# The opening of a two-layer hybrid diffusion trunk: ScalarE copies the modulation rows and takes the norm's root before it splits the first weights

## The chip, the cores and the metric

The kernel runs on one core of a Trainium2 chip. The metric is the device time of one execution in microseconds (us), the median of three runs. The trace is of one execution. Each engine works through its own instructions in program order, and a semaphore wait holds up everything that stands behind it on that engine. In names of rows, PE is TensorE (PEld its weight loads), ACT is ScalarE, DVE is VectorE, POOL is GpSimd, SP is SyncE, which here only issues DMAs; a trailing q is an engine's DMA queue or sequencer.

## The reference

Two layers (`DEPTH` = 2) over 256 context and 512 latent tokens of width 1024. What matters for this change is how layer 0 begins:

```python
sh1x, sc1x, ... = split_cols(silu(c) @ w_ada[l] + b_ada[l], (D_MODEL,) * 6)   # the same of c_ctx
hx = modulate(rms_norm(x, norm_mix_pre[l]), sh1x, sc1x)     # h * (1 + scale) + shift
hc = modulate(rms_norm(h_ctx, norm_mix_pre[l]), sh1c, sc1c)
y_x, y_c = mixing_layer(hx, hc, w_in[l], ...)               # begins with hx @ w_in, hc @ w_in
```

Everything is float32. Behind it stand the three mixers (gated DeltaNet, latent attention, HGRN2), the output projection and an MLP with squared ReLU.

## The kernel before

Activations lie transposed: 8 blocks (`KB`) of 128 features on the partitions by 768 tokens (`TOK`). `X` (residual) is the stream, `Hm` (modulated) its normalised and then modulated form. A float32 product is made of three products of two parts each: `high` is the value cast to fp32r, `low` the rest, and high·high, low·high and high·low are summed.

The order on each engine is written by hand, engine by engine, and semaphores join them. The opening of layer 0 goes like this.

- **SP** issues the constants, the inputs, eight 1 MB loads of modulation weights (`ada_first`, four groups of two halves), the masks, the first three 1 MB loads of `w_in` into a ring of three slots (`weights`), and a copy of `X` to memory (`x_kept`).
- **TensorE** transposes the inputs. Then, for each of the four groups of modulation weights, it multiplies both halves by silu(c) (`ada_half`, L742) into a bank of PSUM. Once ScalarE has copied such a group out as a row (`ada_rows`, L1314), `ada_columns` (L749) turns the row into columns. Between these it sums the squares of `X` over the 1024 features with a matrix of ones (`sum_squares`, L702): blocks 0 to 3 behind group 0, blocks 4 to 7 behind group 1. Then comes the first projection, `gemm_parts` of "qkv" 0 (L672), which for each block k of features waits for `q_low_ready` k+1, and before all for `proj_low_ready` 1.
- **ScalarE** squares the eight blocks (L1327), loads the table for Ln and Exp (`root_tables`, L1237), makes the high part of the first `w_in` weights (`proj_high_part(0, 0)`, L1260, which waits until they have landed), copies two modulation rows, takes the root of the norm as Ln and Exp (`inverse_roots`, L1247 and L1252), copies the other two rows and modulates the eight blocks (`modulate`, L1296, two instructions a block), for which it waits for `mods_ready`.
- **VectorE** makes the low part of the first weights (`proj_low_part`, L1649), multiplies the eight blocks of `X` by the root (`norm_input`, L1636), adds the bias to the modulation columns and makes the gain (L1705, L1715, which raises `mods_ready`), then makes `q_low` for each block (`q_low_block`, L1654).
- **GpSimd** casts each modulated block to its high part (`q_high`, L563), on which `q_low` of that block waits.

Behind the opening, every load into the ring waits for the projection that used the slot last, every projection for its weights' low part, and the convolutions for the projections.

Of the kernel before, what the change touches and what calls it, by code (L numbers as in the profile page):

```python
# [13 lines left out]
KB = D // 128  # L14
# [18 lines left out]
ADA_FIRST = 4  # L33
# [18 lines left out]
def landed(n):  # L52

    return 16 * sum(DMAS.get(what, 1) for _, what, _ in LOADS[n % NSLOT:n + 1:NSLOT])
# [19 lines left out]
def number(table, layer, what, i=0):  # L74

    return layer * len(table) + table.index((what, i))
# [18 lines left out]
def trunk_program(nc, x, ctx, c, c_ctx, w_ada, b_ada, norm_mix_pre, norm_mix_post, norm_mlp_pre, norm_mlp_post,  # L95
# [6 lines left out]
    with stack:  # L102
# [41 lines left out]
        ident, ones, bd64 = kf[:, 0, :], kf[:, 1, :], kf[:, 2, :]  # L144
# [51 lines left out]
        def square_buffer(what, i, n):  # L196

            if what in ("norm0", "norm3"):
                return Y[:, i, :]
            if what in ("norm1", "norm2"):  # L200
                return blocks((2 if what == "norm1" else 0) + i // 4)[:, i % 4, :]
            if what == "l2":
                return X[:, i % 4, :]
            return R[:, 4 if what == "grms" else 6, TOK * (n % 4):TOK * (n % 4 + 1)]
# [30 lines left out]
        def proj_width(s):  # L235

            return 1024 if PROJ[s][0] in ("ba", "ckv") else 2048

        def proj_high(s):

            if s < 7:
                z = R_r[:, 3, 0:2048] if s % 2 else S_r[:, :, :].rearrange("p a b -> p (a b)")
            elif s < 17:
                z = S_r[:, :, :].rearrange("p a b -> p (a b)") if s % 2 else R_r[:, 7, 0:2048]
            else:
                z = R_r[:, s - 15, 0:2048]
            return z[:, 0:proj_width(s)]
# [83 lines left out]
        def lo_of(l):  # L331

            return 0 if l < DEPTH - 1 else CTX
# [4 lines left out]
        def segments(lo):  # L338

            return ([(0, CTX, 1)] if lo == 0 else []) + [(CTX, TOK, 0)]  # L340
# [113 lines left out]
        ada_first = R[:, 1:7, :].rearrange("p a b -> p (a b)")[:, 0:2 * ADA_FIRST * 2048].rearrange("p (i n) -> p i n", n=2048)  # L454
# [182 lines left out]
        def _(pe):  # L637
# [7 lines left out]
            def free_pair(l, what, i=0):  # L645

                n = number(UNITS, l, what, i)
                if n >= 4:
                    pe.wait_ge(gemm_evac, n - 3)
                return pair(n)  # L650

            def streams(lo):
                return ([(0, CTX)] if lo == 0 else []) + [(CTX, TOK)]
# [39 lines left out]
            def sum_squares(l, what, n0, n, mat, lo=0, part=None):  # L693

                dst = free_pair(l, what, n0)
                first = number(SQUARES, l, what, 0 if n > 1 else n0)
                for k in (range(n) if part is None else part):
                    pe.wait_ge(sq_ready, first + k + 1)
                    block = k
                    sq = square_buffer(what, block if n > 1 else n0, first + k)  # L700
                    for a, b in streams(lo):
                        last = mm(dst[:, CTX + a:CTX + b], mat, sq[:, a:b], start=(k == 0), stop=(k == n - 1))  # L702
                    last.then_inc(sq_used, 1)
# [35 lines left out]
            def ada_half(half, w, bank):  # L739

                for k in range(4):
                    last = mm(ps[32 * k:32 * k + 32, bank, :], cs[:, 4 * half + k, :], w[:, k, :], start=(half == 0), stop=(half == 1))  # L742
                return last

            def ada_columns(g, row, col):

                pe.wait_ge(ada_row, g + 1)
                for j in range(4):
                    last = mm(ps[:, 7, col + 2 * j:col + 2 * j + 2], row[:, 128 * j:128 * j + 128], sel[:, :], start=True, stop=True)  # L749
                last.then_inc(ada_tr, 1)  # L750
# [17 lines left out]
            for l in range(DEPTH):  # L768
                lo = lo_of(l)
                if l == 0:  # L770
                    pe.wait_ge(cs_ready, 1)
                    pe.wait_ge(xT_evac, 2 * NC)
                    pe.wait_ge(sel_ready, 1)
                    for g in range(ADA_FIRST):
                        for half in range(2):
                            pe.wait_ge(ada_in[2 * g + half], 16)
                            last = ada_half(half, ada_first[:, 2 * g + half, :].rearrange("p (k n) -> p k n", n=512), 2 + g)
                        last.then_inc(ada_out, 1)
                        if g < 2:
                            sum_squares(l, "norm0", 0, KB, ones, part=range(4 * g, 4 * g + 4))  # L780
                        else:
                            ada_columns(g - 2, ada_first[:, 2 * g - 3, :], 8 * g - 16)
                    for g in range(ADA_FIRST - 2, ADA_FIRST):
                        ada_columns(g, ada_first[:, 2 * g + 1, :], 8 * g)
                else:
                    sum_squares(l, "norm0", 0, KB, ones)
                for i in range(3):
# [406 lines left out]
        def _(act):  # L1194
# [59 lines left out]
            def proj_high_part(l, s):  # L1254

                n = LOADS.index((l, *PROJ[s]))
                act.wait_ge(w_in_s[n % NSLOT], landed(n))
                if 2 <= s < 7 or 9 <= s < 17:
                    act.wait_ge(*weights_used(LOADS.index((l, *PROJ[s - 2]))))
                af(proj_high(s), ring[:, n % NSLOT, 0:proj_width(s)], ACT.Copy).then_inc(proj_high_ready, 1)  # L1260
# [28 lines left out]
            def modulate(l, w, A, B):  # L1289

                if w == 0:
                    act.wait_ge(mods_ready, l + 1)
                for b in range(KB):
                    act.wait_ge(xn_ready, 8 * (2 * l + w) + b + 1)
                    for a, e, s in segments(0 if w == 0 else lo_of(l)):
                        last = af(Hm[:, b, a:e], Hm[:, b, a:e], ACT.Identity, bias=B[:, b, s:s + 1], scale=A[:, b, s:s + 1])  # L1296
                    last.then_inc(h_ready, 1)
# [14 lines left out]
            def ada_rows(g, row, bank):  # L1312
                act.wait_ge(ada_out, g + 1)
                af(row[:, 0:512], ps[:, bank, :], ACT.Copy).then_inc(ada_row, 1)  # L1314
# [6 lines left out]
            for l in range(DEPTH):  # L1321
# [5 lines left out]
                    af(square_buffer("norm0", b, 0), X[:, b, :], ACT.Square).then_inc(sq_ready, 1)  # L1327
                if l == 0:
                    root_tables()
                    proj_high_part(0, 0)  # L1330
                if l == 0:
                    for g in range(2):
                        ada_rows(g, ada_first[:, 2 * g + 1, :], 2 + g)
                inverse_roots(l, [("norm0", 0, D, KB, 0)])
                if l == 0:
                    for g in range(2, ADA_FIRST):
                        ada_rows(g, ada_first[:, 2 * g + 1, :], 2 + g)
                modulate(l, 0, A1, mods[:, l, 0:8, :])
                if l == 0:
                    proj_high_part(0, 1)  # L1340
# [264 lines left out]
        def _(dve):  # L1605
# [38 lines left out]
            def proj_low_part(l, s):  # L1644

                at = slot(l, *PROJ[s])
                dve.wait_ge(proj_high_ready, len(PROJ) * l + s + 1)
                w = proj_width(s)
                v.tensor_tensor(ring_r[:, at, 0:w], ring[:, at, 0:w], proj_high(s), ALU.subtract).then_inc(proj_low_ready, 1)  # L1649
# [58 lines left out]
            for l in range(DEPTH):  # L1708
                lo = lo_of(l)

                def gain(dst, b0, at, plus_one):

                    g = vecs[:, 2 * l, at:at + 8].unsqueeze(2).to_broadcast([128, 8, 2])
                    m = mods[:, l, b0:b0 + 8, :]
                    return (v.scalar_tensor_tensor(dst[:, :, :], m, 1.0, g, ALU.add, ALU.mult) if plus_one  # L1715
                            else v.tensor_tensor(dst[:, :, :], m, g, ALU.mult))
                if l == 0:
                    proj_low_part(l, 0)
                    norm_input(l, "norm0", 0)
                    dve.wait_ge(ada_tr, ADA_FIRST)  # L1720
                    add_bias(0, 0, 16, ps[:, 7, 0:32])
                    gain(A1, 8, V_MIXPRE, True).then_inc(mods_ready, 1)
                    dve.wait_ge(mask_in, 16)
                    for b in range(KB):
                        q_low_block(l, b)
                    proj_low_part(l, 1)
                else:
                    gain(A1, 8, V_MIXPRE, True).then_inc(mods_ready, 1)
                    proj_low_part(l, 0)
                    proj_low_part(l, 1)  # L1730
                    rs = roots(l, "norm0")
                    for b in range(KB + 2):
                        if b < KB:
                            v.tensor_tensor(Hm[:, b, :], X[:, b, :], rs, ALU.mult).then_inc(xn_ready, 1)
                        if b >= 2:
                            q_low_block(l, b - 2)
# [414 lines left out]
```

## Time and profile before

| | |
|---|---|
| median of three runs | 2569.98 us (2568.72 to 2570.99) |
| the profiled execution, first to last instruction | 2553.6 us |
| median less this span | 16.4 us |
| TensorE busy | 2404.3 us, 94% of the span |
| VectorE, ScalarE, GpSimd busy | 1343.5, 860.0, 235.1 us |
| mean granted TensorE clock | 0.981 of full |
| first matmul of the first projection starts | 56.98 us into the span |

The span runs from the first to the last instruction; the device time has 16.4 us around it. The profiled execution's own time as a run is not listed, so a change is counted against its span, and the 16.4 us are taken to stay. The busy share of an engine is an average over the whole kernel; what the opening costs is read from the order of events in its first 60 us.

### The profile page before, as it was taken

To read this page: it belongs to the slowest core of one execution; us is meant where nothing else is said; L and a number is where in the kernel's file an instruction comes from. 1 tells how busy PE (TensorE), PEld (TensorE's weight loads), DVE (VectorE), ACT (ScalarE), POOL (GpSimd) and SP (SyncE) were. 2 spreads that over 40 slices of the span, in tenths; PEclk is the share of its full clock that TensorE was granted. 3 is DMA by queue.
4 is the path that set the end of the run, shared out by engine and by line. 5 is a ranking of instruction groups with operands and counts; after the bars stand their busy time and mean duration, and the time that the engine had idled before them with its cause. 6 is when DMAs were issued, how large, how long until landed. Compare 5 with 4: busy or idle time off the path is not lost.

```text
span 2553.6 us, 34253 instructions
## 1 busy us (share of the span) xinstructions
PE 2404.3 (94%) x14914; PEld 2024.6 (79%) x14914; DVE 1343.5 (53%) x1824; ACT 860.0 (34%) x1197; POOL 235.1 (9%) x188
## 2 busy tenths in 40 slices
PE   6999999999989899999999799999998898999997
PEld 4889797888857688888888587878887756788885
DVE  3689652158654362334333578955228564634444
ACT  5374323210254432122223537343210264322223
POOL 2034300000030020000000013400000030000000
PEclk8999999999999999999999899999999999999998
DMA  8213401122220111122221221431220022233331
GB/s 296 58 51 101 148 11 57 56 77 84 73 99 18 50 50 60 57 66 67 66 66 64 85 58 51 133 116 34 66 81 28 15 99 67 66 99 99 99 99 50
DMA packets 159260, 192.83 MB, mean 76 GB/s; under 512 B 18134, under 2 KB 129080, under 8 KB 158599
## 3 DMA queue, kind: packets, MB, share of 16 engines
q1 hardware_dynamic: 154864, 183.84, 22.2%
q10 hardware_dynamic: 3543, 6.43, 0.8%
q8 instruction: 118, 1.93, 0.3%
q0 software_dynamic: 704, 0.37, 0.1%
q14 instruction: 31, 0.25, 0.0%
HBM read 182.19 MB, written 8.44 MB: 75 GB/s over the span
## 4 chain that ended last, share of the span: by engine, by line
PE 80%; DVE 11%; ACT 4%; issue 2%; SPq 1%; DMA 1%; POOL 0%; DVEq 0%; ACTq 0%
PE ps L1178 33%; PE ps L672 18%; PE ps L1147 4%; PE ps L702 3%; PE ps L1019 2%; PE ps L872 2%; PE ps L878 2%; PE ps L1096 2%; DVE region L1961 1%; PE ps L986 1%; PE ps L1164 1%; DVE region L1992 1%; PE ps L659 1%; PE ps L1109 1%; DVE residual L1856 1%
## 5 line engine op out<-in xcount | busy, mean ns | idle before, releaser
L1178 PE MATMUL ps<-region_r 128*128 128x512 f32 (+1 forms) x1536 | 376.3, 353 | 0.0
L1178 PEld LDWEIGHTS ps<-region_r 128*128 128x128 f32 x1536 | 270.6, 188 | 40.9
L1178 PE MATMUL ps<-region_r,weights_r 128*128 128x512 f32 (+1 forms) x768 | 229.6, 353 | 0.0
L1178 PE MATMUL ps<-mixed_r,region_r 128*128 128x256 f32 (+1 forms) x720 | 215.2, 353 | 0.0
L1178 PE MATMUL ps<-modulated_r,region_r 128*128 128x256 f32 (+1 forms) x720 | 215.2, 353 | 0.0
L1178 PE MATMUL ps<-mixed_r,weights_r 128*128 128x256 f32 (+1 forms) x720 | 215.2, 353 | 0.0
L1642 DVE TENSOR_TENSOR weights_r<-weights,region_r 128x2048 fp32r<-128x2048 f32 x64 | 146.4, 2288 | 118.4 <-ACT region_r L1274 118.4
L1178 PEld LDWEIGHTS ps<-region_r,weights_r 128*128 128x128 f32 x768 | 144.3, 188 | 20.6
L2097 DVE TENSOR_TENSOR region_r<-region 128x768 fp32r<-128x768 f32 (+1 forms) x64 | 52.8, 825 | 204.7 <-ACT region L1582 204.7
L672 PE MATMUL ps<-residual_r,weights_r 128*128 128x256 f32 (+1 forms) x576 | 160.4, 346 | 0.0
L1582 ACT ACTIVATE region<-ps,cst 128x768 f32<-128x768 f32 (+1 forms) x64 | 51.1, 798 | 320.8 <-PE ps L1178 311.3
L1019 PEld LDWEIGHTS ps<-region 128*128 128x128 f32 x1120 | 128.2, 191 | 30.9 <-DVE region L1961 22.5
L1178 PEld LDWEIGHTS ps<-mixed_r,weights_r 128*128 128x128 f32 x720 | 135.3, 188 | 19.2
L1178 PEld LDWEIGHTS ps<-modulated_r,region_r 128*128 128x128 f32 x720 | 135.3, 188 | 19.2
L1178 PEld LDWEIGHTS ps<-mixed_r,region_r 128*128 128x128 f32 x720 | 135.3, 188 | 19.1
L1019 PE MATMUL ps<-region 128*128 128x128 f32 (+1 forms) x1120 | 132.7, 276 | 15.0 <-DVE region L1961 15.0
L1274 ACT ACTIVATE region_r<-weights 128x2048 fp32r<-128x2048 f32 x64 | 122.1, 1908 | 0.0
L672 PEld LDWEIGHTS ps<-residual_r,weights_r 128*128 128x128 f32 x576 | 108.2, 188 | 14.6 <-issue 0.2
L1649 DVE TENSOR_TENSOR weights_r<-weights,state_r 128x2048 fp32r<-128x2048 f32 x18 | 41.2, 2291 | 137.7 <-ACT state_r L1260 137.7
L1588 ACT ACTIVATE region<-ps 128x768 f32<-128x768 f32 (+1 forms) x48 | 33.9, 706 | 215.7 <-PE ps L1178 215.7
L672 PE MATMUL ps<-region_r,state_r 128*128 128x256 f32 (+1 forms) x360 | 90.3, 355 | 14.9 <-DVE region_r L1654 12.1
L672 PE MATMUL ps<-region_r,weights_r 128*128 128x512 f32 (+1 forms) x384 | 104.3, 347 | 0.0
(347 smaller groups left out, 4820.1 us busy)
## 6 DMA issues: line engine op xcount, KB each, us to landing
weights<-in_w_mlp SPq DMA_DIRECT2D x64, 1024.0 KB, 5.4
weights<-in_w_ada SPq DMA_DIRECT2D x40, 1024.0 KB, 5.2
weights<-in_w_in SPq DMA_DIRECT2D x34, 1024.0 KB, 5.2
region<-in_w_ada SPq DMA_DIRECT2D x8, 1024.0 KB, 17.0
weights<-in_w_out SPq DMA_DIRECT2D x8, 1024.0 KB, 6.8
x_kept<-residual SPq DMA_DIRECT2D x2, 3072.0 KB, 12.6
region<-decays_kept ACTq DMA_DIRECT2D x4, 1536.0 KB, 10.6
residual<-x_kept SPq DMA_DIRECT2D x2, 3072.0 KB, 10.8
```

The lines of the kernel that those rows point to most:

```text
L672: last = mm(dst[:, CTX + a:CTX + b], w[:, k, m], r[k][:, a:b], start=(k == 0 and w is high and r is r_high), stop=(k == KB - 1 and r is r_ ...
L702: last = mm(dst[:, CTX + a:CTX + b], mat, sq[:, a:b], start=(k == 0), stop=(k == n - 1))
L872: last = mm(ps[:, ci, 128 * h:128 * h + 128], NT[:, ci, h, :], inverse_alternate(ci, size, h), start=True, stop=True)
L878: last = mm(ps[:, ci, 128 * h:128 * h + 128], W[ci][:, h, :], TT_alternate(ci, size, h), start=True, stop=True)
L1019: last = mm(ps[:, bank, first:first + 64 * ne].rearrange("p (e n s) -> p e n s", e=ne, n=blocks_of), HK[d][:, h, 128 * ci:128 * ci + 128], ...
L1096: last = mm(dst[:, CTX + s0:CTX + s1], QH[0:96, h, 128 * qt:128 * qt + 128], KH[0:96, h, s0:s1], start=True, stop=True)
L1147: last = mm(dst[:, CTX + a:CTX + b], w[:, k, m], r[:, a:b], start=(k == 0 and part_of == "low"), stop=(k == 5 and w is low))
L1178: last = mm(dst[:, CTX + a:CTX + b], w[:, k, m], r[:, a:b], start=(k == 0 and r is r_low), stop=(k == KB - 1 and w is low))
L1274: af(w_high[j % 2], ring[:, n % NSLOT, :], ACT.Copy).then_inc(w_high_ready, 1)
L1582: copied(l, what, u, af(hid[:, b, lo:], src, ACT.Relu, bias=zero_col))
L1642: v.tensor_tensor(ring_r[:, at, :], ring[:, at, :], w_high[j % 2], ALU.subtract).then_inc(w_low_ready, 1)
L2097: v.tensor_tensor(hid_high[:, b, lo:], z, z, ALU.mult)
```

## The change

Three functions change, all for layer 0 and all in the order of the work alone: no instruction is added or left out.

```diff
# TensorE
                         last.then_inc(ada_out, 1)
-                        if g < 2:
-                            sum_squares(l, "norm0", 0, KB, ones, part=range(4 * g, 4 * g + 4))
+                        if g == 0:
+                            sum_squares(l, "norm0", 0, KB, ones)
                         else:
-                            ada_columns(g - 2, ada_first[:, 2 * g - 3, :], 8 * g - 16)
-                    for g in range(ADA_FIRST - 2, ADA_FIRST):
-                        ada_columns(g, ada_first[:, 2 * g + 1, :], 8 * g)
+                            ada_columns(g - 1, ada_first[:, 2 * g - 1, :], 8 * g - 8)
+                    ada_columns(ADA_FIRST - 1, ada_first[:, 2 * ADA_FIRST - 1, :], 8 * ADA_FIRST - 8)
# ScalarE
                 if l == 0:
                     root_tables()
-                    proj_high_part(0, 0)
-                if l == 0:
-                    for g in range(2):
-                        ada_rows(g, ada_first[:, 2 * g + 1, :], 2 + g)
+                    ada_rows(0, ada_first[:, 1, :], 2)
                 inverse_roots(l, [("norm0", 0, D, KB, 0)])
                 if l == 0:
-                    for g in range(2, ADA_FIRST):
+                    for g in range(1, ADA_FIRST):
                         ada_rows(g, ada_first[:, 2 * g + 1, :], 2 + g)
+                    proj_high_part(0, 0)
                 modulate(l, 0, A1, mods[:, l, 0:8, :])
# VectorE
                 if l == 0:
-                    proj_low_part(l, 0)
                     norm_input(l, "norm0", 0)
                     dve.wait_ge(ada_tr, ADA_FIRST)
                     add_bias(0, 0, 16, ps[:, 7, 0:32])
                     gain(A1, 8, V_MIXPRE, True).then_inc(mods_ready, 1)
+                    proj_low_part(l, 0)
                     dve.wait_ge(mask_in, 16)
```

ScalarE's instructions from the squares to the first modulated block, before (the splitting of the first weights is the row `state_r<-weights`, the modulation rows are `region<-ps 128x512`, Ln and Exp the two rows of 128x768 with `cst`):

```order
L1327 ACTIVATE mixed<-residual 128x768 x8
L1237 ACT_TABLE_LOAD
L1260 ACTIVATE state_r<-weights 128x2048
L1314 ACTIVATE region<-ps 128x512 x2
L1247 ACTIVATE region<-ps,cst 128x768
L1252 ACTIVATE region<-region,cst 128x768
L1314 ACTIVATE region<-ps 128x512 x2
L1296 ACTIVATE modulated<-modulated,modulation,pre_gain 128x256
```

and in the changed kernel, whose line numbers are one to three lower:

```order
L1326 ACTIVATE mixed<-residual 128x768 x8
L1236 ACT_TABLE_LOAD
L1313 ACTIVATE region<-ps 128x512
L1246 ACTIVATE region<-ps,cst 128x768
L1251 ACTIVATE region<-region,cst 128x768
L1313 ACTIVATE region<-ps 128x512 x3
L1259 ACTIVATE state_r<-weights 128x2048
L1295 ACTIVATE modulated<-modulated,modulation,pre_gain 128x256
```

One row copy and Ln and Exp now stand ahead of the weights, as do the other three row copies; the weights stand directly ahead of the modulation.

VectorE's instructions from the end of the constants to `q_low`, before:

```order
L1701 TENSOR_TENSOR lower_bound<-lb_tmp 128x8
L1649 TENSOR_TENSOR weights_r<-weights,state_r 128x2048
L1636 TENSOR_TENSOR modulated<-residual,region 128x768 x8
L1705 TENSOR_TENSOR modulation<-ps,vecs 128x32
L1715 SCALAR_TENSOR_TENSOR pre_gain<-modulation,vecs 128x16
L1654 TENSOR_TENSOR region_r<-modulated,region_r 128x768 x4
```

and now:

```order
L1698 TENSOR_TENSOR lower_bound<-lb_tmp 128x8
L1633 TENSOR_TENSOR modulated<-residual,region 128x768 x8
L1702 TENSOR_TENSOR modulation<-ps,vecs 128x32
L1712 SCALAR_TENSOR_TENSOR pre_gain<-modulation,vecs 128x16
L1646 TENSOR_TENSOR weights_r<-weights,state_r 128x2048
L1651 TENSOR_TENSOR region_r<-modulated,region_r 128x768 x4
```

The low part of the weights (`weights_r<-weights,state_r`) has moved from ahead of the norm to between the gain and the first `q_low`.

TensorE's instructions from the second half of the sum of squares to the first projection (each block has two matmuls of L702, and an instruction in float32 stands once here and in several passes in the trace), before:

```order
L702 MATMUL ps<-mixed,k_f_sb 128x256
L702 MATMUL ps<-mixed,k_f_sb 128x512
L702 MATMUL ps<-mixed,k_f_sb 128x256
L702 MATMUL ps<-mixed,k_f_sb 128x512
L742 MATMUL ps<-region,silu_c 32x512 x8
L749 MATMUL ps<-row_select,region 128x2 x4
L742 MATMUL ps<-region,silu_c 32x512 x8
L749 MATMUL ps<-row_select,region 128x2 x12
L672 MATMUL ps<-region_r,state_r 128x256
```

and now:

```order
L702 MATMUL ps<-mixed,k_f_sb 128x512
L702 MATMUL ps<-mixed,k_f_sb 128x256
L702 MATMUL ps<-mixed,k_f_sb 128x512
L742 MATMUL ps<-region,silu_c 32x512 x8
L749 MATMUL ps<-row_select,region 128x2 x4
L742 MATMUL ps<-region,silu_c 32x512 x8
L749 MATMUL ps<-row_select,region 128x2 x4
L742 MATMUL ps<-region,silu_c 32x512 x8
L749 MATMUL ps<-row_select,region 128x2 x8
L672 MATMUL ps<-region_r,state_r 128x256
```

Group 1 (one `region,silu_c` row) has moved from the middle of the sum to behind it, and each group's columns (`row_select,region`) now follow one group later, not two.

## Rows read from the trace of the kernel before

**Rows 1.** The page, part 4: the whole span's chain that ended last, by engine.
```profile
PE 80%; DVE 11%; ACT 4%; issue 2%; SPq 1%; DMA 1%; POOL 0%; DVEq 0%; ACTq 0%
```

**Rows 2.** ScalarE's timeline: start, length, instruction, [idle before it <- what ended that].
```profile
21.97 5.98 ACT L1327 ACTIVATE mixed<-residual 128x768 f32<-128x768 f32 x8
27.97 1.28 ACT L1237 ACT_TABLE_LOAD   x1
...
49.24 0.60 ACT L1314 ACTIVATE region<-ps 128x512 f32<-128x512 f32 x1 [2.60 <-PE ps L742]
53.58 9.71 ACT L1296 ACTIVATE modulated<-modulated,modulation,pre_gain 128x256 f32<-128x256 f32 x16 [3.74 <-DVE pre_gain L1715]
```

**Rows 3.** The chain that ended last, in order of time: start us, us, what.
```profile
23.45 2.58 SPq L464
...
28.70 12.79 DMA weights<-in_w_in
...
41.51 1.91 ACT state_r L1260
...
44.40 0.80 ACT region L1247
...
45.22 0.95 ACT region L1252
...
46.19 7.04 DVE modulated L1636 x8
...
53.58 1.31 ACT modulated L1296 x2
...
54.94 0.83 POOL region_r L563
...
55.87 0.97 DVE region_r L1654
...
56.98 77.80 PE ps L672 x432
```

**Rows 4.** TensorE's timeline, 20 to 60 us.
```profile
23.89 5.43 PE L702 MATMUL ps<-mixed,k_f_sb 128*128 128x256 f32 x16
...
31.11 5.43 PE L702 MATMUL ps<-mixed,k_f_sb 128*128 128x256 f32 x16
36.46 1.92 PE L742 MATMUL ps<-region,silu_c 128*32 128x512 f32 x16
43.96 1.87 PE L749 MATMUL ps<-row_select,region 128*128 128x2 f32 x8 [5.57 <-ACT region L1314]
45.76 3.40 PE L742 MATMUL ps<-region,silu_c 128*32 128x512 f32 x16
49.09 2.84 PE L749 MATMUL ps<-row_select,region 128*128 128x2 f32 x24
```

**Rows 5.** DMA issues: the last of w_ada, and x_kept: number, KB each, median us from issue to landing.
```profile
region<-in_w_ada SPq DMA_DIRECT2D x1, 1024.0 KB, 14.2
...
x_kept<-residual SPq DMA_DIRECT2D x1, 3072.0 KB, 16.1
```

**Rows 6.** GpSimd's timeline, 53.5 to 58.2 us.
```profile
56.14 1.38 POOL L563 CAST region_r<-modulated 128x768 fp32r<-128x768 f32 x1 [0.37 <-ACT modulated L1296]
...
57.47 0.83 POOL L563 CAST region_r<-modulated 128x768 fp32r<-128x768 f32 x1
```

**Rows 7.** VectorE's timeline, 56.2 to 60 us.
```profile
57.55 1.54 DVE L1654 TENSOR_TENSOR region_r<-modulated,region_r 128x768 fp32r<-128x768 f32 x1 [0.72 <-POOL region_r L563]
```

**Rows 8.** Busy time and granted TensorE clock (PEclk, 1.00 is full) in stretches.
```profile
core 0: us, PE busy (x) PEld busy (x) DVE busy (x) ACT busy (x) POOL busy (x), PEclk, DMA share, GB/s
...
42.00:44.00 2.00, 0.04 (x1) 0.04 (x1) 0.47 (x1) 2.00 (x3) 0.00 (x0) 0.50 1.10 349
52.00:54.00 2.00, 0.00 (x0) 0.00 (x0) 1.50 (x4) 0.42 (x1) 0.00 (x0) 0.55 0.27 115
...
62.00:64.00 2.00, 2.00 (x12) 1.74 (x11) 2.00 (x3) 2.00 (x4) 2.00 (x2) 0.89 0.03 8
```

## The prediction, made before the changed kernel ran

> **What bounds the kernel now.** I read the chain that ended last, first for the whole span and then for the first 60 us. Over the whole span TensorE holds 80% of it [rows 1], and from 56.98 us on it runs through 432 projection matmuls in one piece of 77.80 us [rows 3]. What the opening decides is thus when that piece starts. The chain ahead of it is: the landing of the first `w_in` weights at 28.70 + 12.79 = 41.49; their high part on ScalarE, 1.91; two row copies, Ln and Exp; the norm on VectorE from 46.19, 7.04; the modulation of block 0 from 53.58, 1.31; GpSimd's cast, 0.83; VectorE's `q_low`, 0.97; then TensorE [rows 3].
>
> The engines' timelines show that Ln had no need to wait for that landing. ScalarE ended the squares at 21.97 + 5.98 = 27.95 and the table load at 29.25, then had nothing to do until 41.51 [rows 2, 3]. TensorE ended the sum of squares at 31.11 + 5.43 = 36.54 and group 2 at 38.38, then stood still for 5.57 us until a modulation row had been copied [rows 4]. Ln stood behind the weights in ScalarE's order, and so did the rows that TensorE waited for.
>
> **The change, part by part.** The arithmetic is the same. I follow the new order with the old durations.
>
> *TensorE.* Group 0 ends as before, and the sum starts at 23.89. Its second half takes 36.46 - 31.11 = 5.35 from start to start [rows 4], so both halves take 10.7 and end at 34.6, with the last result out at 34.7. The squares finish at 27.95, ahead of it. Group 1 runs 34.6 to 36.5 (1.9, as group 2 in [rows 4]). The columns of a group are a third of 24 matmuls in 2.84, so 0.95 [rows 4]. Then: columns 0 to 37.4, group 2 to 39.3, columns 1 to 40.2, group 3 to 42.1, columns 2 to 43.1, columns 3 to 44.0. The last half of group 3 was issued at 23.45 and landed 14.2 later [rows 3, 5], at 37.65, so it is there. Each row is copied while TensorE does something else: row 0 at 29.3, row 1 behind Exp at 36.5, row 2 at 39.3, row 3 at 42.2 to 42.8 (0.60 each [rows 2]).
>
> *ScalarE and the norm.* Ln starts at 34.7, where it started at 44.40. From its start to the norm's are 46.19 - 44.40 = 1.79 [rows 3], so the norm runs 36.5 to 43.6. Now it ends 0.4 ahead of the columns, and these become the later of the two. From the norm's end to the modulation were 53.58 - 53.23 = 0.35 [rows 3]; from 44.05 that gives `mods_ready` at about 44.4. But ScalarE has taken the weights at 42.8 (they landed at 41.49), and for 1.9 they hold the modulation behind them: it starts at **44.65**, 8.9 earlier than 53.58. The weights thus cost 0.25 on the path here; they cost 1.9 before.
>
> *VectorE's low part of the weights* was hidden: it ended under Ln and Exp. Now it stands between the gain and `q_low` 0, and starts with the end of the high part, 44.65 to 44.8. Its duration is not in my rows of the chain, so I bound it by them: 2048 columns where a `q_low` of 768 takes 0.97 [rows 3], hence up to 2.6, and 2.3 when 0.1 of each is a fixed cost. It ends at about 47.1. Before, `q_low` 0 came 55.87 - 53.58 = 2.29 behind the modulation's start; 44.65 + 2.29 = 46.9. Without more, it would now start at 47.1, and the gain at TensorE would be 8.9 - 0.15 = about 8.7.
>
> *The two engines that meet there.* GpSimd's cast of block 0 wants to start at 44.65 + 1.36 = 46.0, in the middle of that low part. The trace shows what such a meeting costs. The cast at 56.14 began during `q_low` 0 (55.87 to 56.84) and took 1.38, where one alone takes 0.83; it ended at 57.52, 0.7 behind the end of the VectorE instruction [rows 3, 6]. And `q_low` 1, at 57.55, took 1.54 against 0.97, because the cast at 57.47 (0.83, to 58.30) had come first [rows 6, 7]. So I take it that one stands until the other has ended. Then cast 0 ends at 47.1 + 0.7 = 47.8, cast 1 follows at once (its block is ready at 44.65 + 2.5), and `q_low` 0, which starts at 47.8, takes the 1.54 of `q_low` 1 and ends at 49.3. TensorE started 56.98 - 56.84 = 0.14 behind that: **49.5**, which is 7.5 earlier. The bounds of this term: nothing, with the gain 8.7 to 8.9; and 1.4, the one I take, as both meetings have a row like them. If a cast lost only the 0.55 that the row shows, it would end at 47.4 and the gain would be 7.9.
>
> The Trainium skill, "SBUF — State Buffer", section "Who interferes with whom", says that a VectorE instruction with two inputs in SBUF and a GpSimd instruction that reads SBUF exclude each other, the second to issue standing until the first has ended. By that rule the cast stands behind the whole 2.3 us low part, not only for the 0.55 of the row, and the sum would be 7.5 and not 7.9. The two casts of the row agree with it, but no row here has a cast behind so long an instruction.
>
> *TensorE's clock.* It was full until 52.2, 0.3 us after TensorE's last matmul, then half (mean 0.55 over 52 to 54), and full again from about 62.4 (mean 0.89 over 62 to 64) [rows 8]. So the first projection ran its first 5.5 us at half clock and lost 2.7. In the new order TensorE stands still from 44.0 to 49.5, 5.5 us against 5.05, so I expect the same fall and the same loss; 0 is my value, with a bound of 1 us either way for when the clock comes back. The gaps ahead of it, which had group 3 at 3.40 and not 1.92 [rows 4], close.
>
> *Behind the opening.* The second `q_low` follows 1.5 after the first, and TensorE takes longer than that per block at half clock, so VectorE doesn't hold it. `x_kept` is issued at 38.41 as before and lands 16.1 later [rows 5], at 54.5; VectorE asks for it behind eight `q_low` and one low part, at 49.3 + 7 x 1.5 + 2.3 = 62. Every later load waits for a projection, so it moves with them. I take the whole 7.5 as passed on.
>
> Sum: 2553.6 - 7.5 = 2546.1 for the span; with the same 16.4 around it, 2562.5 against the median of 2569.98, 0.29% less.
>
> **The rivals.**
> 1. *The meeting costs nothing* (cast and low part run side by side): gain 8.7 to 8.9, 2561.2. Against it stand both long rows of [rows 6, 7]. An earlier return of the clock comes to the same side: up to 2.7 more, were it full from the first matmul. Chance of this side: 0.17.
> 2. *The clock falls during the columns.* The one fall that [rows 8] hold came right behind 24 column matmuls of 2 columns each, on a TensorE that was busy all through them. The new order has such matmuls from 36.5 on, a third of the time. If the clock fell at about 41, group 3 would take up to 1.5 more and the two column steps behind it 0.85 each (43.96 to 45.76 for 8 against 0.95 [rows 4]). Columns 3 would end at 47.2, the modulation start at 47.6 with the low part behind it as before: 3.0 given back, gain 4.5, 2565.5. For the forecast speaks that two thirds of that stretch is full-width work, as ahead of 38.38. Chance 0.14.
> 3. *The change doesn't do what it says.* The gain in the opening is made, and a later wait takes it back, so that the time stays at 2570. That needs an event tied to the clock on the wall and not to the projections; I found none but `x_kept`, which has 7 us to spare. Chance 0.05.
> 4. *Slower: the weights' landing.* ScalarE now waits for `w_in` 0 directly ahead of the modulation, and the eight blocks stand behind that wait. Landed at 41.49, it costs nothing before 42.8; from there each us costs one. It decides from 42.8 + 7.5 = 50.3 on, 8.8 later than it landed. With a landing of 52.8 the kernel would take 2572.5 or more, if its earlier form did not share the delay. The transfers ahead of it are the same. Chance 0.04.
>
> **How the numbers follow.** Forecast (gain 6.5 to 8.5): 0.60. Rivals: 0.17, 0.14, 0.05, 0.04. What a measurement of this kernel can tell from no change is about 0.2%, 5.1 us. Faster by more: 0.60 + 0.17 + a little of rival 2 = 0.79. Within: 0.17. Slower: 0.04. The range goes down to 2560.0 (rival 1 with some of the clock) and up to 2566.5 (rival 2 with 1 us of spread between runs, which was 2568.72 to 2570.99).
>
> **What would show it.** Right: the first L672 matmul at 49.5 (49 to 50), the norm from 36.5, the modulation from 44.65, a cast of 1.7 or so that ends 0.7 behind the low part, full clock from 34 to 44, and all later events earlier by one and the same amount. Wrong: a cast 0 of 0.83 (rival 1), a group 3 of over 2.5 us (rival 2), a wait after 60 us that is longer than before (rival 3), or a wait of ScalarE for `w_in` (rival 4).

## The result: faster by more than was forecast, and outside the range

Over 22 runs of each, the changed kernel took 2554.36 us (median; 2543.17 to 2571.28) and the kernel before 2569.35 us (2555.23 to 2585.39). The ratio is 0.9945, 95% interval 0.9925 to 0.9966: 14 us less, where 7.5 were forecast, and below the range's lower end of 2560.0. Counted over all runs of this study (162 of before with a mean of 2566.5, one more of 3488.25 us at a clock of 0.647 left out; 70 of the changed kernel with a mean of 2555.2) it is **11.3 us, with 2.4 either way** (1.96 times the root of the summed squares of the standard errors, 0.7 and 1.0). That interval takes every run as independent. The sets that the runs came in differ by more than this allows (below, "Both kernels again"); counted over the means of the seven sets of before and the five of the changed kernel, it is 11.6 with 3.5 either way.

The opening in the trace of the changed kernel went nearly as predicted. Its page begins and its chain by engine reads:

```profile
span 2547.5 us, 34253 instructions
...
PE 81%; DVE 11%; ACT 3%; issue 2%; DMA 1%; SPq 1%; POOL 0%; DVEq 0%; ACTq 0%
```

The chain that ended last (start us, us, what), beside [rows 3]:

```profile
28.82 13.63 DMA weights<-in_w_in
42.50 1.79 issue
44.30 1.30 ACT modulated L1295 x2
45.60 0.05 issue
45.65 1.76 POOL region_r L563
47.46 0.04 issue
47.50 1.48 DVE region_r L1651
48.98 0.14 issue
49.12 77.04 PE ps L672 x432
```

Ln, Exp and the norm are gone from the chain. The piece of 432 projection matmuls starts at 49.12 and not at 56.98, 7.86 earlier, and takes 77.04 (77.80 in [rows 3]). It is shorter because the clock came back sooner behind its start: it was 0.50 over 48 to 52 us, 0.76 over 52 to 54 and 1.00 over 54 to 56, so that some 3.9 us ran at half clock, where [rows 8] give 5.5 before.

ScalarE's timeline shows what took their place:

```profile
28.57 0.60 ACT L1313 ACTIVATE region<-ps 128x512 f32<-128x512 f32 x1
33.84 0.90 ACT L1246 ACTIVATE region<-ps,cst 128x768 f32<-128x768 f32 x1 [4.67 <-PE ps L702]
...
41.39 0.60 ACT L1313 ACTIVATE region<-ps 128x512 f32<-128x512 f32 x1 [2.24 <-PE ps L742]
42.48 1.91 ACT L1259 ACTIVATE state_r<-weights 128x2048 fp32r<-128x2048 f32 x1 [0.49 <-DMA weights<-in_w_in]
44.30 9.68 ACT L1295 ACTIVATE modulated<-modulated,modulation,pre_gain 128x256 f32<-128x256 f32 x16
```

Ln now waits for the sum of squares, as it should, and the weights still end the chain, since they landed at 42.45 here. The wait is 0.49 us: rival 4's mechanism, in a small form. VectorE's timeline:

```profile
35.81 7.04 DVE L1633 TENSOR_TENSOR modulated<-residual,region 128x768 f32<-128x768 f32 x8 [19.23 <-ACT region L1251]
43.24 0.19 DVE L1702 TENSOR_TENSOR modulation<-ps,vecs 128x32 f32<-128x32 f32 x1 [0.39 <-PE ps L749]
...
44.42 2.29 DVE L1646 TENSOR_TENSOR weights_r<-weights,state_r 128x2048 fp32r<-128x2048 f32 x1 [0.78 <-ACT state_r L1259]
```

and TensorE's, beside [rows 4]:

```profile
23.21 10.59 PE L702 MATMUL ps<-mixed,k_f_sb 128*128 128x256 f32 x32
33.73 1.92 PE L742 MATMUL ps<-region,silu_c 128*32 128x512 f32 x16
35.58 1.05 PE L749 MATMUL ps<-row_select,region 128*128 128x2 f32 x8
...
39.40 1.92 PE L742 MATMUL ps<-region,silu_c 128*32 128x512 f32 x16
41.26 1.95 PE L749 MATMUL ps<-row_select,region 128*128 128x2 f32 x16
```

Group 3 takes 1.92 (3.40 in [rows 4]). The clock over 34 to 44 us was 1.00 (the columns are those of [rows 8]):

```profile
34.00:44.00 10.00, 9.20 (x80) 4.89 (x72) 7.41 (x10) 4.98 (x6) 0.00 (x0) 1.00 1.08 359
```

So the opening gained 7.9, where 7.5 were forecast. The profiled execution as a whole gained 2553.6 - 2547.5 = 6.1. The experiments ask two things: whether each step of the opening is what it was taken for, and where the other 3 to 6 us come from (11.3 over all runs, 14 in the 22 of the result). Theory 1: the change is worth what it takes off the start of the first projection; the rest is chance between executions. Theory 2: the new order also saves falls of the TensorE clock behind the opening. I told them apart by repeats of both kernels and by kernels with the new order and the old start.

### The profile page after: what moved, and what is told of

Its sections match the earlier page's. It is cut to its first block, busy times and chain, and to the rows that moved or that the text cites. A ratio compares the mean times of both kernels' runs of the same rounds, so it can differ in the third digit from the quotient of the medians.

```text
span 2547.5 us, 34253 instructions
## 1 busy us (share of the span) xinstructions
PE 2403.7 (94%) x14914; PEld 2025.2 (79%) x14914; DVE 1343.4 (53%) x1824; ACT 858.9 (34%) x1197; POOL 237.0 (9%) x188
## 4 chain that ended last, share of the span: by engine, by line
PE 81%; DVE 11%; ACT 3%; issue 2%; DMA 1%; SPq 1%; POOL 0%; DVEq 0%; ACTq 0%
PE ps L1177 33%; PE ps L672 18%; PE ps L1146 4%; PE ps L702 2%; PE ps L871 2%; PE ps L1018 2%; PE ps L877 2%; PE ps L1095 2%; DVE region L1958 1%; PE ps L985 1%; PE ps L1163 1%; DVE region L1989 1%; PE ps L659 1%; PE ps L1108 1%; DVE residual L1853 1%
## 5 line engine op out<-in xcount | busy, mean ns | idle before, releaser
L672 PE MATMUL ps<-residual_r,region_r 128*128 128x256 f32 (+1 forms) x352 | 100.7, 353 | 0.0
```

The lines of the kernel that those rows point to most:

```text
L672: last = mm(dst[:, CTX + a:CTX + b], w[:, k, m], r[k][:, a:b], start=(k == 0 and w is high and r is r_high), stop=(k == KB - 1 and r is r_ ...
```

## The experiments

### VectorE's low part back in front of the norm

```diff
                 if l == 0:
+                    proj_low_part(l, 0)
                     norm_input(l, "norm0", 0)
 ...
                     gain(A1, 8, V_MIXPRE, True).then_inc(mods_ready, 1)
-                    proj_low_part(l, 0)
```

> The changed kernel with VectorE's low part of the first weights back in front of the norm. It starts when the high part ends (44.3) and ends at 46.7, the norm runs to 53.8 and the gain behind it to 54.2, so the modulation starts at 54.2 and the first projection at 57.6 instead of 49.1. Theory 1: 0.6 us above the kernel before. Theory 2: some 6 below it, since ScalarE and TensorE keep the new order. If VectorE's place did not matter, the projection would start at 49.

The mean of 12 runs is 2567.0, 0.6 above that of before, with 5.0 either way (ratio to the runs beside it 1.0011, 0.9988 to 1.0035). The chain in its trace:

```profile
41.27 0.60 ACT region L1313
41.87 1.81 ACT state_r L1259
...
43.78 2.29 DVE weights_r L1646
46.07 6.95 DVE modulated L1633 x8
...
53.36 1.31 ACT modulated L1295 x2
...
55.65 0.97 DVE region_r L1651
56.62 0.14 issue
56.76 3.54 PE ps L672 x10
```

The norm stands behind the low part, which waits for weights that ScalarE splits at 41.77, though its root was ready at 35.6. All but 0.2 of the opening's gain is gone, counted against the first trace of before (56.98). The part on VectorE is thus not a detail: without it the other two gain nothing in the opening, and nothing that 12 runs can show. I had put the projection at 57.6; it came at 56.76, because the high part ended at 43.68 here and not at 44.3, and the modulation started at 53.36 and not at 54.2. From there to the projection are the 3.40 that I had assumed. Theory 1 expected 0.6 above before, theory 2 some 6 below: the mean is where theory 1 had it, with 5.0 either way. Whether the parts on ScalarE and TensorE are both needed was not run.

### The cast of block 0 on ScalarE

```diff
# GpSimd
                 for b in range(KB):
+                    if l == 0 and b == 0:
+                        pool.wait_ge(q_high_ready, 1)
+                        continue
                     pool.wait_ge(h_ready, 16 * l + b + 1)
# ScalarE, in modulate
                     last.then_inc(h_ready, 1)
+                    if l == 0 and w == 0 and b == 0:
+                        act.wait_ge(h_ready, 1)
+                        af(q_high[0], Hm[:, 0, :], ACT.Copy).then_inc(q_high_ready, 1)
```

> The changed kernel with the cast of block 0 on ScalarE instead of GpSimd, so that no cast meets VectorE's low part. If the two engines shut each other out, as predicted: the low part ends at 46.7, q_low 0 follows at once and takes 0.97, the first projection starts at 47.9 instead of 49.1, 1.2 us off the time. If the meeting costs nothing, the projection stays at 49.1.

> The changed kernel with the cast of block 0 on ScalarE, a second set of runs. From the start of the modulation to the first projection 3.44 us again, where the changed kernel takes 4.82. On average over both sets 1.4 us below the changed kernel, which the spread of the runs may hide.

ScalarE's timeline in the first of them:

```profile
44.34 1.30 ACT L1298 ACTIVATE modulated<-modulated,modulation,pre_gain 128x256 f32<-128x256 f32 x2
45.67 0.84 ACT L1302 ACTIVATE region_r<-modulated 128x768 fp32r<-128x768 f32 x1
```

VectorE's:

```profile
44.47 2.29 DVE L1652 TENSOR_TENSOR weights_r<-weights,state_r 128x2048 fp32r<-128x2048 f32 x1 [0.18 <-ACT state_r L1262]
46.68 0.95 DVE L1657 TENSOR_TENSOR region_r<-modulated,region_r 128x768 fp32r<-128x768 f32 x1
```

and TensorE's:

```profile
47.78 0.98 PE L675 MATMUL ps<-region_r,state_r 128*128 128x256 f32 x2 [3.92 <-DVE region_r L1657]
```

From the modulation's start to the first projection are 3.44 us in both sets (44.34 to 47.78, 43.40 to 46.84), and 4.82 in the changed kernel (44.30 to 49.12). `q_low` 0 takes 0.95 and follows the low part at once; in the changed kernel it took 1.48 and stood behind a cast of 1.76. The meeting of the two engines costs **1.38 us**; 1.4 was the term. The times can't show it: 24 runs have a mean of 2555.7 against 2555.2, a difference of 0.5 with 3.8 either way (ratios to before 0.9984, 0.9962 to 1.0007, and 0.9940, 0.9915 to 0.9965). No version here is measurably faster than the changed kernel.

### Both kernels again

The same two kernels without an edit, on two chips.

> The kernel before itself, once more, to see how far its own runs spread and where the TensorE clock falls in another execution. Theory 1 (the change is worth its 7.9 us in the opening, the rest of the measured 14 is chance in the clock's falls): ratio 1.000 with an interval of some 0.5% either way, a first projection at 56 to 58 us, and falls of the clock at other places than in the first trace. Theory 2 (the change also saves falls of the clock behind the opening): the same ratio, but the falls at the same places as in the first trace.

> The changed kernel itself, once more. Theory 1: first projection at 49 us, 7.5 to 8.5 below the kernel before on average, with an interval that holds 7.9. Theory 2: some 14 below, and in its trace fewer stretches at half clock behind 60 us than in traces of the kernel before.

> The kernel before, a third set of runs, for the mean over more executions and one more trace. Theory 1 (the change is worth what it takes off the start of the first projection, 7.9 us): no difference from the other runs of the kernel before than chance gives, some 2.3 us for the mean of a dozen. Its trace: from the first projection to the end 2495 to 2520 us, the long ones with more time at half clock.

> The changed kernel, a third set of runs. Theory 1: over all its runs, against all runs of the kernel before, some 8 us less (9 over the sets so far). Theory 2 (some 6 us more are saved behind the opening): 14 less. From the first projection to the end in the trace: the same 2495 to 2520 us as in traces of the kernel before under theory 1, about 6 us less than there on average under theory 2.

> The kernel before, a fourth set. So far its 116 runs have a mean of 2567.0, the changed kernel's 46 one of 2556.0, 11.1 apart, with 3.0 either way. Theory 1 (the gain is what the opening gains, and in three traces of each kernel the transposes of the decay inputs at the end of the opening come 8.5 us earlier on average): with more runs the difference comes down towards 8.5. Theory 2 (more is saved behind the opening): it stays at 11 or above. Its opening: transposes at 133.5 to 137.5 us.

> The changed kernel, a fourth set, for the same question as the fourth set of the kernel before. Transposes at 126 to 128 us. Theory 1: mean of the set 2558.5 within 5. Theory 2: 2556 or less.

> The changed kernel, a fifth set, for the same question. Transposes at 126 to 128 us. Theory 1: mean of the set 2558.5 within 5. Theory 2: 2556 or less.

| set | runs | mean us | ratio to the runs of before beside it (95%) | first projection | transposes behind it | traced span |
|---|---|---|---|---|---|---|
| before, first trace | 22 | 2570.3 | | 56.98 | 134.69 | 2553.6 |
| before, again | 12 | 2570.0 | 1.0025 (1.0001 to 1.0049) | 57.19 | 133.76 | 2571.7 |
| before, third | 12 | 2564.2 | 0.9998 (0.9973 to 1.0024) | 59.36 | 137.41 | 2566.1 |
| before, fourth | 12 | 2564.9 | 1.0011 (0.9989 to 1.0032) | 57.69 | 136.33 | 2574.2 |
| changed | 22 | 2556.2 | 0.9945 (0.9925 to 0.9966) | 49.12 | 126.08 | 2547.5 |
| changed, again | 12 | 2559.7 | 0.9990 (0.9968 to 1.0012) | 48.50 | 126.08 | 2544.7 |
| changed, third | 12 | 2551.9 | 0.9946 (0.9920 to 0.9972) | 50.34 | 128.17 | 2547.3 |
| changed, fourth | 12 | 2553.1 | 0.9952 (0.9931 to 0.9974) | 48.27 | 125.51 | 2549.2 |
| changed, fifth | 12 | 2554.5 | 0.9951 (0.9924 to 0.9978) | 48.57 | 126.42 | 2556.4 |

Beside these sets ran three more of the kernel before, of 35, 35 and 34 runs, without a trace that was kept: their means are 2562.7, 2569.3 and 2565.1. With them the kernel before has its 162 runs.

Three things follow. First, a set of a dozen runs says little: the means of the sets spread over 7 us for one and the same kernel, single runs over 30, and the kernel before against itself gave 1.0025 with an interval that leaves out 1 (2570.0 against 2562.7 beside it). The seven means of before lie further apart than the spread of the runs within them gives, so something that a whole set shares moves the time, by some 2 to 3 us as an estimate from these means, and intervals that count single runs are too narrow. What it is, no run shows. The 14 of the result are the high side of all this.

The expectations came out like this. In the repeat of the changed kernel the ratio, 0.9990, was nearer to theory 1: its interval ends at 0.9968, 8.2 us below before, where theory 2 wanted 14. The difference over all runs, which under theory 1 was to come down to 8.5, went from 11.1 to 11.3. For the fourth and fifth set 2558.5 was expected under theory 1 and 2556 or less under theory 2; they came at 2553.1 and 2554.5. On these two counts theory 2 did better.

Second, the opening itself gains more on average than in the one pair of traces. The first projection starts at 57.8 (mean of four) and at 49.0 (mean of five): **8.8 us, with 1.3 either way**, and 9.1 at the transposes that end the opening. Against the 56.98 of the first trace, the mean of before is 0.8 later. Two things make this up. One is the landing of the first weights: ScalarE took them at 41.51, 41.73, 42.39 and 42.23 in the four traces, 0.5 later on average than in the first, and the old chain moves with them. The other stands in the third trace of before alone, in TensorE's timeline:

```profile
46.64 3.64 PE L742 MATMUL ps<-region,silu_c 128*32 128x512 f32 x16
50.21 5.28 PE L749 MATMUL ps<-row_select,region 128*128 128x2 f32 x24
```

and in the busy times and the clock of two stretches (columns as in [rows 8]):

```profile
45.00:50.00 5.00, 5.00 (x24) 2.21 (x24) 4.63 (x5) 2.48 (x4) 0.00 (x0) 0.50 1.06 446
50.00:55.00 5.00, 5.00 (x27) 4.79 (x23) 4.11 (x5) 0.60 (x1) 0.00 (x0) 0.50 0.49 208
```

The clock stayed at half through group 3 and all columns. They took 8.85 and not the 6.17 of [rows 4] from group 3's start to the last column, the columns became later than the norm, and the modulation started at 55.96, 2.4 later than in [rows 2]; 0.9 of this is the later landing of the weights, the other 1.5 the columns. In the other three traces group 3 took 3.40 to 3.64, the 24 column matmuls 2.84 to 3.02, and the norm stayed the later of the two. In all five traces of the changed kernel this stretch ran at full clock, and the last 16 column matmuls took 1.95. The new order is not free of the clock, though: in its third trace group 0, ahead of the sum, took 3.64 at half clock, the sum began at 24.76 and the projection at 50.34.

Third, what lies between the first projection and the end differs from execution to execution of one kernel: 2496.6, 2514.5, 2506.7 and 2516.5 us before, 2498.4, 2496.2, 2496.9, 2500.9 and 2507.9 in the changed kernel. The means are 8.5 apart, with 9.8 either way. Theory 1 expected no difference and theory 2 about 6, so this count leans to theory 2 and decides nothing. The traces show two reasons for the long ones.

One is time at half clock. A stretch of the first trace of before (columns as in [rows 8]):

```profile
290.00:320.00 30.00, 25.92 (x350) 21.95 (x349) 14.33 (x30) 16.70 (x32) 4.08 (x4) 1.00 0.52 175
```

and the same of its second trace:

```profile
290.00:320.00 30.00, 25.86 (x303) 20.78 (x301) 10.71 (x21) 15.54 (x29) 2.04 (x2) 0.77 0.52 174
```

The clock was 1.00 in one and 0.77 in the other, and TensorE got through 303 matmuls for 350 in the same 30 us. Most falls come at the same places of the program: counted from the first projection, all nine traces have one that starts at 342 to 348 us, and again at 684 to 693, 820 to 829, 838 to 847 and 1384 to 1398. The expectation for the first repeat had called this a sign of theory 2, but the changed kernel has the same places, so it doesn't tell the theories apart. How long the falls last, and whether some further places (near 239 and 1640 us) have one, differs from execution to execution, in both kernels. Behind the opening the record of the clock has 73, 127, 76 and 109 us at half clock before, and 76, 86, 83, 100 and 116 in the changed kernel. The means, 96 and 92, are 4 us apart, which at half clock is worth 2 us at most. So the traces don't show that the new order saves more than that.

The other reason is not the clock. Here are 400 us in the matmuls of the MLP (L1178), from the first trace of before:

```profile
950.00:1350.00 400.00, 400.00 (x2309) 352.73 (x2308) 136.15 (x112) 84.52 (x72) 0.00 (x0) 1.00 0.20 64
```

and from its third:

```profile
950.00:1350.00 400.00, 400.00 (x2266) 347.00 (x2265) 132.54 (x111) 83.48 (x71) 0.00 (x0) 1.00 0.20 62
```

TensorE was busy without a gap and at full clock in both, and yet did 2% less in the third. Between 850 and 1380 us behind the first projection this cost 10.0 us, which is all of the third trace's 10.1 above the first. The fourth trace of before has the same 2266 and lost 10.0 there, the kernel whose low part stands first has 2266 too, and the other eleven traces of this study have 2309 or 2310. What sets it, no run shows. It came in three of the seven traces whose first projection starts at 56 us or later and in none of the seven that start earlier, which may be chance.

### The new order with the old start

```diff
# ScalarE, proj_high_part
+                if l == 0 and s == 0:
+                    for _ in range(4):
+                        link(af(proj_high(s), ring[:, n % NSLOT, 0:proj_width(s)], ACT.Copy))
                 af(proj_high(s), ring[:, n % NSLOT, 0:proj_width(s)], ACT.Copy).then_inc(proj_high_ready, 1)
```

> The changed kernel whose ScalarE makes the high part of the first weights five times instead of once (the same values each time), 4 x 1.94 = 7.8 us more ahead of the modulation, so that the new order stands but the first projection starts at 56.9 again. Theory 1: the whole gain is gone, the mean is that of the kernel before within some 2.5 us. Theory 2 (the order itself saves something behind the opening): some 6 us of it stay.

> The changed kernel with the high part of the first weights made five times, a second set. Transposes at 134 us as before. Theory 1: with the first set a mean within 3.5 us of the kernel before. Theory 2: 2.5 us or more below it.

Its chain, first set:

```profile
42.21 1.92 ACT state_r L1261
44.13 0.02 issue
44.15 1.92 ACT state_r L1261
...
51.79 1.30 ACT modulated L1298 x2
53.09 0.06 issue
53.15 1.76 POOL region_r L563
...
56.62 3.54 PE ps L672 x10
```

The projection starts at 56.62 and 56.22, on average 7.5 later than in the changed kernel. The 24 runs have a mean of 2563.1 (sets of 2565.2 and 2561.0; ratios to before 0.9989, 0.9958 to 1.0020, and 0.9994, 0.9973 to 1.0015). That is 7.9 above the changed kernel, with 4.0 either way (4.9 when counted over sets): with its start the changed kernel loses what the start took off. Against the kernel before it is 3.4 less, with 3.7 either way (4.7 over sets), of which its start explains 1.4 (56.4 against 57.8). The first set is where theory 1 had it. The second fits both: 3.4 is within the 3.5 of theory 1 and beyond the 2.5 of theory 2. Taken with the kernel whose low part stands first (2567.0, projection at 56.76), 36 runs with the new TensorE order and the old start have a mean of 2564.4, 2.1 below before with 3.1 either way (4.0 over sets), of which the start explains 1.3. A saving of 6 us that stays with the order when the start is lost is excluded, one of 2 is not. One that needs the early start and the order together, these kernels can't show.

## Why the prediction was wrong

*Ln behind the sum.* Right. Forecast 34.7, measured 33.84 with a sum that began 0.68 earlier; from there to the norm 1.97 against the 1.79 assumed. The 1.79 was a reading of the chain, where a piece starts at the end of the one ahead of it; in ScalarE's timeline of before, Ln starts at 44.28, 1.91 ahead of the norm.

*The columns become the later of two.* Right: VectorE waited 0.39 us for them, forecast 0.4.

*The weights ahead of the modulation.* Right in place: 44.30 for 44.65. But what set it was the landing, at 42.45 in this execution and not 41.49, and not the row copy ahead of it. In the changed kernel's second trace ScalarE started on them at 41.86, as soon as the row was copied. The two stand within some 0.5 us of each other.

*The low part on the path, and the meeting.* Right in each number. The low part took 2.29 (2.3), the cast that came in the middle of it took 1.76 and ended at 47.41, 0.70 behind it (0.7), and `q_low` 0 took 1.48 (1.54). With the cast elsewhere 1.38 came back (1.4). The Trainium skill, "SBUF — State Buffer", section "Who interferes with whom", had the cast stand behind the whole low part; here it did, and 0.55, the longest delay that a row of before had shown, would have been too little (0.93 was measured).

*TensorE's clock, and the trace as typical.* Wrong in size. I took one trace of before as its typical opening. Over four traces the old opening starts the projection at 56.98 to 59.36, from later landings of the weights and, once, from columns at half clock, and the opening is worth 8.8 and not 7.5. The bound of 1 us on the clock's return held in the first pair of traces: the clock came back 1.6 us sooner behind the start, which gave 0.8. Rival 2, a fall during the columns, did not happen in any of the traces of the new order.

*Sum and range.* Here is the step that failed: the median of 2569.98 was taken as the time of the kernel, "with the same 16.4 around it", and the range allowed "1 us of spread between runs". In every run the time is the span and 1.8 us (2549.32 for 2547.5), so that the traced execution of before took about 2555.4. It was among the fastest tenth of its kernel. The 16.4 were not something around the span, but mostly what other executions had beyond this one: time at half clock, and in two of the three other traces the 10 us of the slower stretch at full clock. In the forecast they cancel, since they were in the median to begin with; what doesn't cancel is the spread that they stand for. The three runs shown, 2568.72 to 2570.99, happened to lie close; 162 have a standard deviation of 8.3 and a mean of 2566.5.

The forecast of 2562.5 was 8.1 above the measured median. Of these, 3.5 come from the three runs, which lay above the mean of their kernel; 1.3 from the opening, 8.8 for 7.5; 0.8 from the 22 runs of the changed kernel, which lay below its mean; and 2.5 are the rest of the 11.3. With the right mean and the opening alone the forecast would have been 2557.7, below the range's end of 2560.0. The direction and the opening were right by their mechanism; how far outside the range the median fell is in part luck.

The rest of 2.5 has 2.4 either way from the runs, 3.5 when counted over sets, and the 8.8 has 1.3 of its own. It may be chance, a small saving in clock falls behind the opening, or the slower stretch of the MLP coming less often. Its cause stays open.

## What to carry to other kernels

An in-order engine that waits for a transfer should have ahead of that wait everything that does not need the transfer; but look on every engine, since here the change on ScalarE and TensorE took 0.2 us off the opening while VectorE kept the old order. When a piece of work moves from under cover to the path, look at what the other engine does at that moment: 2.29 us of low part on VectorE met a cast on GpSimd and cost 1.38 more than its length. And before a gain of some us is read from one trace and three runs, find out how far executions of the same kernel differ, and compare means over dozens of runs in several sets. The device time less the span of the same execution is a constant here (1.8 us); a median less the span of another execution is not.

## What the runs showed of the hardware

One kernel varies by some 30 us in 2560 from execution to execution, and the time goes with the granted clock: over the 22 runs of the changed kernel the correlation is -0.87, from 2543.17 us at 0.985 to 2571.28 us at 0.974. The mean clock is not all of it: the first and the third trace of before have 0.981 and 0.980 and are 12.5 us apart, 10.0 of them in one stretch in which TensorE was busy throughout at full clock and did 2266 matmuls for 2309. The clock of TensorE also stayed at half through 8.85 us in which it was busy throughout, with 24 of its 40 matmuls 2 columns wide, and stayed full where 8 such matmuls at a time took turns with 16 that were 512 columns wide (33.73 to 43.21 in the changed kernel's trace).
